# The opening of a diffusion step: the first block of h is multiplied ahead of the second modulation group

## What is computed

```
def block(x, cond, lp, ctx=None):
    sh1, sc1, gt1, sh2, sc2, gt2 = ada_mod(cond, w_ada, b_ada)   # silu(cond) @ w_ada + b_ada, split in six
    h = rmsnorm(x, g_mix) * (1 + sc1) + sh1
    gq, gk, gv, gr, zf, zb, nq, nk, nv, m_gla, m_na = split_in(h @ w_in)
    ...                                    # gated linear attention over 4 heads, both directions
    ...                                    # neighbourhood attention over 8 heads
    mix = (jax.nn.sigmoid(m_gla) * b_gla + jax.nn.sigmoid(m_na) * b_na) @ w_out
    x = x + gt1 * mix
    h2 = rmsnorm(x, g_ffn) * (1 + sc2) + sh2
    x = x + gt2 * conv_ffn(h2, w_up, w_conv, b_conv, w_down)
    return x, (kn, vn, s_f, s_b)
```

## Time and profile before

| | before |
|---|---|
| median of 3 runs | 1001.97 us |
| lowest, highest | 1001.19, 1002.47 us |
| the profiled execution: time, span | 1002.16 us, 1000.4 us |
| TensorE busy | 975.5 us, 98% of the span |
| VectorE, ScalarE, GpSimd busy | 605.5, 448.8, 510.0 us |
| mean granted clock of TensorE | 0.998 |

### The profile page before, as it was taken

How to read it: one execution, slowest core, us unless ns; L and a number is a source line. 1 busy time by engine, 2 the same in 40 slices (tenths; PEclk the granted TensorE clock), 3 DMA queues, 4 the chain that set the end, 5 groups by cost and what they waited for, 6 DMA issues and landing times.

```text
span 1000.4 us, 18178 instructions
## 1 busy us (share of the span) xinstructions
PE 975.5 (98%) x7139; PEld 907.9 (91%) x7139; DVE 605.5 (61%) x1091; ACT 448.8 (45%) x696; POOL 510.0 (51%) x361
## 2 busy tenths in 40 slices
PE   3999999999999999999999999999999999999998
PEld 3999999999788889999988899999999999888886
DVE  7407348973476657934764899777777778913002
ACT  4244263542576665442432365555555556611110
POOL 1465842212333322774560457888888886433331
PEclk9999999999999999999999999999999999999999
DMA  9978213122001103488871122222222231322231
GB/s 339 313 84 88 82 46 81 44 64 68 28 23 43 43 23 96 128 260 274 280 270 35 43 86 85 85 85 85 86 85 85 85 95 54 127 80 68 94 124 56
DMA packets 132076, 105.51 MB, mean 105 GB/s; under 512 B 6902, under 2 KB 112283, under 8 KB 131739
## 3 DMA queue, kind: packets, MB, share of 16 engines
q1 hardware_dynamic: 127112, 97.32, 32.8%
q0 software_dynamic: 1568, 3.15, 2.2%
q10 hardware_dynamic: 3315, 3.94, 1.1%
HBM read 99.91 MB, written 3.42 MB: 103 GB/s over the span
## 4 chain that ended last, share of the span: by engine, by line
PE 86%; DVE 6%; issue 3%; SPq 1%; POOL 1%; ACT 1%; DMA 1%; DVEq 0%; POOLq 0%; ACTq 0%
PE PJ L886 8%; PE PJ L887 7%; PE PJ L891 7%; PE PA L1478 6%; PE PA L1480 6%; PE PA L1479 6%; PE PA L1367 3%; PE PA L1368 3%; PE PA L1369 3%; PE PJ L1367 3%; PE PJ L1368 3%; PE PJ L1369 3%; PE PA L1210 2%; PE PJ L1193 2%; PE PA L1024 2%
## 5 line engine op out<-in xcount | busy, mean ns | idle before, releaser
L672 POOL TENSOR_TENSOR wlo<-wraw,whi 128x1024 fp32r<-128x1024 f32 x54 | 135.1, 2504 | 272.3 <-ACT whi L1531 182.4
L886 PE MATMUL PJ<-h_hi,whi 128*128 128x320 f32 x512 | 158.0, 316 | 0.4 <-ACT qk_rs L1686 0.4
L887 PE MATMUL PJ<-h_lo,whi 128*128 128x320 f32 x512 | 154.4, 309 | 0.0
L891 PE MATMUL PJ<-h_hi,wlo 128*128 128x320 f32 x512 | 116.8, 309 | 0.0
L886 PEld LDWEIGHTS PJ<-h_hi,whi 128*128 128x128 f32 x512 | 96.4, 188 | 3.2 <-issue 1.4
L887 PEld LDWEIGHTS PJ<-h_lo,whi 128*128 128x128 f32 x512 | 96.5, 188 | 0.0
L891 PEld LDWEIGHTS PJ<-h_hi,wlo 128*128 128x128 f32 x512 | 85.8, 188 | 0.0
L1531 ACT ACTIVATE whi<-wraw 128x1024 fp32r<-128x1024 f32 x39 | 40.9, 1050 | 57.9 <-PE PJ L891 51.6
L2028 ACT ACTIVATE whi<-wraw 128x1024 fp32r<-128x1024 f32 x21 | 22.3, 1060 | 98.6 <-PE PA L1369 51.6
L843 POOL TENSOR_TENSOR behind<-behind_val,behind 128x512 fp32r<-128x512 f32 x40 | 52.1, 1302 | 19.0 <-ACT behind L2007 19.0
L1480 PE MATMUL PA<-h_hi,behind 128*128 128x320 f32 x192 | 59.3, 309 | 0.0
(11 more groups left out here) (548 smaller groups left out, 3109.8 us busy)
## 6 DMA issues: line engine op xcount, KB each, us to landing
wraw<-in_w_in_dram SPq DMA_DIRECT2D x74, 256.0 KB, 3.1
ada_rest<-in_w_ada_dram SPq DMA_DIRECT2D x32, 512.0 KB, 5.8
wraw<-in_w_up_dram SPq DMA_DIRECT2D x48, 256.0 KB, 3.8
wraw<-in_w_down_dram SPq DMA_DIRECT2D x42, 256.0 KB, 2.9
raw_even<-in_w_up_dram SPq DMA_DIRECT2D x40, 256.0 KB, 3.6
ada<-in_w_ada_dram SPq DMA_DIRECT2D x8, 1024.0 KB, 10.6
out_dram<-x ACTq DMA_DIRECT2D x10, 256.0 KB, 2.0
x_rows<-in_x_sample_dram SPq DMA_DIRECT2D x2, 1024.0 KB, 6.6
```

The source lines that it names most:

```text
L672: pool.tensor_tensor(wlo[:, slot, 0:k, :], wraw[:, slot, 0:k, :], whi[:, slot, 0:k, :].bitcast(F32), ALU.subtract).then_inc(lo_done, 1)
L886: pe.matmul(out, whi[:, slot, w0 + k, :], hi(k)[:, tok], start=start and k == k0, stop=False)
L887: pe.matmul(out, whi[:, slot, w0 + k, :], lo(k)[:, tok], start=False, stop=False)
L891: mm = pe.matmul(out, wlo[:, slot, w0 + k, :], hi(k)[:, tok], start=False, stop=stop and k == k1 - 1)
```

## The change

`modulation_rows(1)` moves from ahead of the loop over the blocks into it, behind the two tiles of block 0. `rows_to_columns(1)` moves from behind block 0 to a place within block 1, between `first_tile(0, 1)` and `first_tile(1, 1)`.

```
             modulation_rows(0)
             rows_to_columns(0)
-            modulation_rows(1)
             pe.wait_ge(xt_cp_act, 3)
             pe.wait_ge(xt_cp_dve, 2)
             for k in range(NK):
                 for n in (0, 1) if k < NK - 1 else (1, 0):
                     first_tile(n, k)
+                    if (n, k) == (0, 1):
+                        rows_to_columns(1)
                 if k == 0:
-                    rows_to_columns(1)
+                    modulation_rows(1)
                 if k in (1, 3):
                     modulation_rows(k // 2 + 2)
                     for past in (k - 1, k):
```

## The result

The changed kernel is slower: median 1003.79 us (1002.46 to 1005.59, 20 runs) against 1002.08 us (1000.96 to 1003.94, 20 runs), 1.7 us. The ratio is 1.0018, 95% interval 1.0012 to 1.0024. I had forecast 1001.4 us with a range of 1000.2 to 1002.6, and a change that can't be told from none. The measured median lies 1.2 us above that range, and the kernel moved the other way.

The account below looks back on a forecast made before the run. TensorE's own line of work, its waits and its clock were taken to bound the kernel. The third group's landing capped the gain at 0.62 us: 1001.97 to 1001.35, rounded 1001.4 us, range 1000.2 to 1002.6.

Parts of the forecast that it names:

- The restart: Before the first block: TensorE, waiting for h_lo instead of the DMA, restarts at 25.17 instead of 25.93, 0.76 us earlier.
- The second group's rows without a wait: Behind block 0's two tiles: the second group's data has been there 1.1 us by 26.93, so that wait is gone.
- the turn for nothing: Second group's turn, behind block 1's first tile: that tile's 0.88 us covers VectorE's 0.29 us copy; TensorE doesn't wait.
- The third group's landing caps the gain, whatever the clock does: Third group's rows: data lands at 32.58, rows start at 32.71 instead of 33.33, gain 0.62 us in both clock courses.
- two courses: Opening: clock low 3.4 us as before, or not falling, with arrival 1.6 us earlier; both wait for the third group, 0.62 us.
- Rival (b): Third group's landing: the kernel before also waits there when its clock doesn't fall, so gain 0, 1002.0 us; 19%.
- Rival (c): New wait for the third group: clock falls behind it, rows and tiles run slower, +1.07 us, 1003.0; 8%.
- (a): Third group lands before TensorE arrives, no cap: gain 0.76 us (1001.2) or 2.45 (999.5); 10%.
- (d): First tile still waits, for its low weights or the copies of xT: no gain, 1002.0 us; 3%.
- The shift is kept to the end: Behind the third group's rows nothing turns later, so the 0.62 us gain goes through to the kernel's end.

Follow-up runs that it names:

- filler ahead of the transposes: Changed kernel plus 22 small unused-result matmuls in TensorE's two waits before the transposes: 1002.75 us; with 12 matmuls behind the first turn too: 1001.95.
- 6 fillers: Changed kernel plus 6 matmuls of unused result in TensorE's wait between first turn and first block: 1002.23 us, ratio 1.0001 to the kernel before.
- the turn alone: Kernel before with only the second group's turn moved behind the first tile of block 1, its rows staying ahead (also "turn only"): 1002.09 us, ratio 1.0000.
- before, 2nd: Second profile of the unchanged kernel before, nothing altered: span 1000.7 us, restart at 24.60 us.
- before, late: Kernel before with one wait more: the second group's rows also wait for the first block's h_lo: 1003.05 us, ratio 1.0012.
- 12 fillers: Changed kernel plus 12 matmuls of unused result in TensorE's wait between first turn and first block: 1001.38 us, ratio 0.9996 to the kernel before.
- the kernel before with filler: Kernel before plus 12 matmuls of unused result behind the first turn: 1001.63 us, ratio 0.9997.

## Why the prediction was wrong, step by step

**The restart (the first move), wrong.** I took 25.17 in place of 25.93. Measured: 26.33 and 26.36 in place of 24.60 and 25.01, with 25.93 once. Both sides came from one execution, and it was unusual in both.

The block came early in it. TensorE's middle eight transposes start at the same time in this profile and in that of the kernel after, but take twice as long in the second:

```profile
16.74 1.04 PE L912 MATMUL PA<-ident,x_rows 128*128 128x128 f32 x8
```

```profile
16.74 1.91 PE L912 MATMUL PA<-ident,x_rows 128*128 128x128 f32 x8
```

The trace's record of the clock begins at 16.60 in the first and at 18.80 in the second. The view shows 1.00 ahead of that too, where nothing is recorded; by the durations TensorE was at the lower level there. In the twelve profiles without filler ahead of the transposes the first turn follows this time: it stands at 21.8 to 22.0 where the record begins near 16.6 (three profiles), and at 22.4 to 23.6 where it begins at 17.8 to 19.9 (nine). So the time of the clock's first rise set, by and large, when the first block was ready: 25.13 in the first profile of the kernel before, 25.67 and 26.87 in its two others.

And the data came late in it. The second half of the second group took 10.61 us to land; in ten of the 14 profiles it took 9.3. The kernel after has it handed over at 15.04, and of this transfer:

```profile
ada<-in_w_ada_dram SPq DMA_DIRECT2D x1, 1024.0 KB, 9.3
```

It landed at 24.3, while TensorE waited for the block until 26.33; in the old order it could have begun on the rows at about 24.5, an estimate from this landing and the 0.13 us of the earlier trace rows. By the same sum the block could be begun ahead of the data in two of the 14 profiles only, the first of the kernel before and that with 6 fillers. The sign of this term was wrong as a rule: the change replaces a wait that ends at about 24.6 by one that ends at 26.3, 1.7 us of idle time more. Of the forecast 25.17, another 0.2 is the handing over of 0.25 us taken at 0.05.

**The second group's rows without a wait, and the turn for nothing: right.** The rows follow the tiles without a gap, and the turn alone measures 1.0000.

**"The third group's landing caps the gain, whatever the clock does": the cap is right, the clause is wrong.** The cap shows in eight profiles, as a start of the third group's rows between 32.29 and 32.65 behind a wait. I weighed two courses, a low stretch of 3.4 us and none, and let the first cost the same after as before. The measured one was neither, 6.8 us, and it costs more than the cover. From the restart to the third group's rows the changed kernel needs 35.13 - 26.33 = 8.80 us; with filler 32.04 - 25.98 = 6.06. The low clock costs 2.74 us, and at the full clock TensorE would have been there at 32.39, about when the DMA lands (starts at 32.29 to 32.65). This is the step that failed: the clock's loss, taken at 1.69 us as before or at nothing, and called harmless either way, measured 2.74 us and was not covered. The Trainium skill, TensorE: Matmul & The Clock Gate, section Terms, puts the penalty at the throttled time by the share that is missing: 6.84 x 0.5 = 3.4 us here, an estimate from that page. The trace has 2.74. TensorE was waiting anyway in the first 0.7 us of the low stretch, which leaves 3.1, and its work there took less than twice its time: 3.47 us for two tiles against 1.93. The bound of about 358 GB/s from HBM that I had set beside the landing (the Trainium skill, DMA: Bandwidth & Descriptors, section Where 436 GB/s comes from) doesn't agree with the kernel after either: its stretches from 27 to 35 us moved 381 to 390 GB/s.

**Rival (b), right for the kernel before in its end, only in part in its reason, too low in chance.** I had argued that an execution before in which the clock doesn't fall would also run into the cap, and gave it 19% as a way to a zero. The third profile is of that kind; in the second the clock fell, and it reached the cap because it restarted 1.3 us earlier. So two of its three profiles show the cap, and so do the turn alone and one of the two late ones, which have the old order. It is why the kernel before pays for its own low stretch only in part: by the medians filler takes 0.45 us from it, within the noise, and 2.0 to 2.4 from the changed one.

**Rival (c), right in kind.** A clock that falls behind a wait for the third group was seen once, in the old order. What made the changed kernel slower was the clock too, but at the wait ahead of the first block, where I let only the loss of before be repeated. I had looked for an idle time between 1.0 and 3.7 us from which the clock falls. The length alone doesn't decide it: the clock fell behind 1.80 us (before, 2nd) and 2.00 us (turn only), and held through 3.04 us (before, late). Rivals (a) and (d) didn't occur: no third group's rows started ahead of 32.29, and in the kernel after the first tile waited for `h_lo` alone.

**The shift is kept to the end: right.** The two profiles of before and after differ by 1.80 at the third turn, and by 1.69 on VectorE at 842 us:

```profile
840.96 0.49 DVE L2753 TENSOR_TENSOR u_all<-tmp,PA 128x320 f32<-128x320 f32 x1 [1.27 <-PE PA L1480]
```

```profile
842.65 0.49 DVE L2754 TENSOR_TENSOR u_all<-tmp,PA 128x320 f32<-128x320 f32 x1 [1.27 <-PE PA L1481]
```

The first row is of before, the second of after. The spans differ by 2.8; the last 1.0 is the late effect below, which the second profile of the kernel before has as well.

**The sum.** Third turn after: 38.86. Before: 37.07, 36.39, 36.19, on the average 36.55. The difference of these few profiles, 2.3, is somewhat above the 1.7 of the timed runs. With the clock held only 0.2 is left of it (12 fillers: 36.40 after, 36.21 before), less than the landing varies from profile to profile. So the loss is the low clock. That it is the later restart which brings it on is shown in part only, by the kernel before restarted late: slower by 1.0 us, with the rows still first.

**What stays open.** Why the clock stayed low for 6.8 us in three profiles and for 3.4 in the others. In the three, tiles came first and TensorE restarted 0.7 to 1.3 us after the fall. With the rows first and a restart 0.6 after the fall it was 3.4, and so it was where TensorE worked at the fall already, with tiles or rows. By the timed runs lateness has a part, whatever the work: a mean clock of 0.996 stands beside 12 of 81 runs of the kernel before, five of 11 with the late restart on the rows, and 26 of 31 of the changed kernel. A single stretch of 3.4 us goes with 0.998 in every profile; whether 0.996 is one long stretch or two short ones a timed run doesn't tell. Whether the kind of work adds to it isn't settled, nor why the clock fell in some executions of a kernel and not in others.

The fastest version that the runs point to is the changed kernel with 12 fillers, 1001.38; its ratio to the kernel before, 0.9996, isn't clear of 1. The cap at 32.3 to 32.7 leaves no more in this place, as long as the third group lands when it does.

## What to carry to other kernels

A wait that TensorE makes for one thing hides what else would be late there. Before trading one for the other, read both ends in several executions: the restart on the data and the block's end, 25.9 and 25.1 in one profile, were 24.6 and 25.7, and 25.0 and 26.9, in two more of the same kernel. Idle time of TensorE can have a second price, the clock: here it fell in eight of the ten profiles without filler in the wait, behind waits of 1.8 to 3.7 us, came back after 3.4 or 6.8 us, and cost up to 2.7 us of work that was otherwise covered. Throwaway matmuls in such a wait are a cheap test for that price, and here also the cure.

## What the runs showed besides

GpSimd's subtraction of line 672 takes 2.7 us near 868 us in seven profiles and 6.35 to 6.37 us in the other seven, whatever the kernel. GpSimd in the two profiles of the kernel before with the same work (start, duration):

```profile
868.42 2.73 POOL L672 TENSOR_TENSOR wlo<-wraw,whi 128x1024 fp32r<-128x1024 f32 x1 [4.64 <-ACT whi L2028]
```

```profile
867.67 6.37 POOL L672 TENSOR_TENSOR wlo<-wraw,whi 128x1024 fp32r<-128x1024 f32 x1 [4.65 <-ACT whi L2028]
```

TensorE then waits 0.80 us for it, a wait that the first does not have:

```profile
874.09 0.50 PE L1367 MATMUL PA<-whi,act_mid 128*128 128x512 f32 x1 [0.80 <-POOL wlo L672]
```

This goes with the 1.0 us between 963.3 and 964.3 above: the same seven profiles have both. The runs of the kernel before with filler stand in two heaps as far apart, seven at 1001.05 to 1001.66 and four at 1002.42 to 1002.71; that this effect splits them is likely, but a timed run doesn't show it. Beside the long subtraction SyncE's four loads of line 599 take 11.82 us to be issued instead of 8.17; which of the two holds up the other was not tried.

The third group's data landed with the rows at 32.3 to 32.7 in every kernel whose TensorE was early enough to wait for it, a spread of 0.4 us; the second group's landing varied from 24.3 to 25.8 over all profiles.
